# Wide and narrow expert passes, one after the other or mixed unit by unit

## Reference

```python
D_FF_EXPERT = 3584; N_EXPERTS = 8; TOP_K = 2
def swiglu(x, w_gate, w_up, w_down):
    return (jax.nn.silu(x @ w_gate) * (x @ w_up)) @ w_down

def moe_swiglu(x, router_w, w_gate, w_up, w_down):
    logits = (x @ router_w).astype(jnp.float32)
    top_v, top_i = lax.top_k(logits, TOP_K)
    gates = jax.nn.softmax(top_v, axis=-1)
    combine = jnp.sum(jax.nn.one_hot(top_i, N_EXPERTS, dtype=jnp.float32) * gates[..., None], axis=-2)
    y = jnp.zeros_like(x)
    for e in range(N_EXPERTS):
        y = y + combine[..., e:e + 1].astype(x.dtype) * swiglu(x, w_gate[e], w_up[e], w_down[e])
    return y
```

## Time and profile before

| | |
|---|---|
| three runs | 2547.36, 2551.19, 2551.25 us (median 2551.19) |
| profiled execution | 2547.49 us, span 2545.5 us |
| busy: PE, PEld, DVE, ACT | 2435.9, 2106.4, 1891.4, 1407.5 us (96, 83, 74, 55%) |
| DMA | 593.18 MB, mean 233 GB/s |
| chain of waits, by engine | PE 67%, DVE 21%, DMA 5% |
| segment `moe` (seven straight passes) | 1593.7 to 2392.0 us |
| pass 7 in `over` | 2392 to 2528 us |

### The profile page before, as it was taken

How to read it: one execution, slowest core, us unless ns; L and a number is a source line. 1 busy time by engine, 2 the same in 40 slices (tenths; PEclk the granted TensorE clock), 3 DMA queues, 4 the chain that set the end, 5 groups by cost and what they waited for, 6 DMA issues and landing times.

```text
span 2545.5 us, 36256 instructions
## 1 busy us (share of the span) xinstructions
PE 2435.9 (96%) x14462; PEld 2106.4 (83%) x14462; DVE 1891.4 (74%) x2230; ACT 1407.5 (55%) x1546; POOL 0.2 (0%) x4
## 2 busy tenths in 40 slices
PE   7999999999999999989999988999999999999897
PEld 7999889899998998886998886787777777888786
DVE  7665755567657454976544985889999999988787
ACT  4654443456445343223442322678888888777574
POOL 0000000000000000000000000000000000000000
PEclk9999999999999999999999998999999999999998
DMA  6334455344345544304544302899999999999796
GB/s 260 133 117 149 163 217 199 134 156 144 122 153 210 184 166 170 130 34 158 191 165 152 133 17 99 329 362 403 412 413 413 413 411 413 383 342 371 287 354 260
DMA packets 119622, 593.18 MB, mean 233 GB/s; under 512 B 17440, under 2 KB 17824, under 8 KB 77472
## 3 DMA queue, kind: packets, MB, share of 16 engines
q1 hardware_dynamic: 110224, 585.40, 60.4%
q10 hardware_dynamic: 9232, 5.47, 0.8%
HBM read 589.79 MB, written 1.05 MB: 232 GB/s over the span
## 4 chain that ended last, share of the span: by engine, by line
PE 67%; DVE 21%; DMA 5%; issue 4%; ACT 3%; SPq 0%; DVEq 0%; ACTq 0%; POOLq 0%
PE bank L608 21%; PE bank L2508 17%; PE bank L865 12%; DVE wlo L687 7%; DMA ring<-in_stream 4%; PE bank L1717 3%; DVE big L2963 2%; DVE ring_lo L839 2%; PE bank L1133 2%; ACT whi L682 1%; PE bank L1148 1%; PE bank L1738 1%; PE bank L1903 1%; DVE big L2125 1%; PE bank L2448 1%
## 5 line engine op out<-in xcount | busy, mean ns | idle before, releaser
L687 DVE TENSOR_TENSOR wlo<-ring,whi 128x2048 fp32r<-128x2048 f32 x430 | 979.1, 2290 | 112.3 <-ACT whi L682 108.6
L682 ACT ACTIVATE whi<-ring 128x2048 fp32r<-128x2048 f32 x433 | 825.4, 1912 | 109.4 <-PE bank L2508 50.0
L2508 PE MATMUL bank<-whi,xhi 128*128 128x512 f32 x896 | 366.8, 409 | 16.4 <-DVE wlo L687 12.3
L2508 PE MATMUL bank<-wlo,xhi 128*128 128x512 f32 x896 | 352.2, 393 | 0.0
L839 DVE TENSOR_TENSOR ring_lo<-ring,slot_hi 128x1024 fp32r<-128x1024 f32 x160 | 192.4, 1222 | 130.2 <-ACT slot_hi L816 123.1
L608 PE MATMUL bank<-xhi,whi 128*128 128x256 f32 x864 | 245.8, 284 | 2.5 <-DVE xlo L570 1.3
L608 PE MATMUL bank<-xlo,whi 128*128 128x256 f32 x864 | 245.7, 284 | 0.0
L608 PE MATMUL bank<-xhi,wlo 128*128 128x256 f32 x864 | 245.6, 284 | 0.0
L816 ACT ACTIVATE slot_hi<-ring 128x1024 fp32r<-128x1024 f32 x160 | 166.5, 1052 | 107.2 <-PE bank L865 77.6
L2508 PEld LDWEIGHTS bank<-whi,xhi 128*128 128x128 f32 x896 | 170.0, 190 | 63.9 <-DVE wlo L687 30.5
L865 PE MATMUL bank<-xh,slot_hi 128*128 128x256 f32 x704 | 202.5, 288 | 3.0 <-DVE ring_lo L839 3.0
(11 more groups left out here) (524 smaller groups left out, 4505.8 us busy)
## 6 DMA issues: line engine op xcount, KB each, us to landing
ring<-in_stream SPq DMA_DIRECT2D x555, 1024.0 KB, 7.3
par<-in_par ACTq DMA_DIRECT2D x2, 2048.0 KB, 10.0
con<-in_con SPq DMA_DIRECT2D x1, 1216.0 KB, 10.6
X<-in_x SPq DMA_DIRECT2D x2, 512.0 KB, 4.1
out_y<-X SPq DMA_DIRECT2D x2, 512.0 KB, 2.6
par<-in_par ACTq DMA_DIRECT2D x2, 448.0 KB, 6.2
par<-in_par ACTq DMA_DIRECT2D x2, 157.5 KB, 4.4
con<-in_con SPq DMA_DIRECT2D x1, 64.0 KB, 4.3
```

What stands on the lines that cost most here:

```text
L682: act.activation(whi[:, k % NSPLIT, :], src, ACT.Copy).then_inc(act_done, AC.step(tag + f".w{k}"))
L687: v.tensor_tensor(wlo[:, k % NSPLIT, :], src, whi[:, k % NSPLIT, :].bitcast(F32), ALU.subtract)\
L2508: mm = pe.matmul(out, left, right, start=start and i == 0, stop=stop and i == len(pairs) - 1)
```

## The change

`TRACKS` names two tracks, (0, 5, 6, 7) wide and (1, 2, 3, 4) narrow. `straight_units` mixes the units of the two in the segment `moe`: `STRETCHES` gives pairs (wide units, narrow units), and within a pair they are spread evenly. The order of the 98 units (W wide, n narrow) is

The small order work of DVE (`v_order_passes`) moves from units 1 to 3 to units 0, 5 and 7, and the table of experts for SP is written in its first part. The rolled segment keeps its own side work in banks 6 and 7. Core of the diff:

```diff
-WIDE_PASS = (0, 5, 6, 7)
+TRACKS = ((0, 5, 6, 7), (1, 2, 3, 4))
+WIDE_PASS = TRACKS[0]
+STRETCHES = ((5, 0), (9, 9), (4, 5), (5, 14), (5, 4), (7, 10), (7, 3), (0, 11))
...
             def turn(g):
-                if g >= 2:
-                    pe.wait_ge(vec_done, VE.at(tag + (f".hl{g - 2}" if is_wide(g - 2, rolled) else f".h{g - 2}")))
+                if g:
+                    pe.wait_ge(vec_done, VE.at(tag + (f".hl{g - 1}" if is_wide(g - 1, rolled) else f".h{g - 1}")))
...
+            aside_read = []
+
+            def side(kind, p, piece):
+                for done, steps, name in aside_read[-1:]:
+                    pe.wait_ge(done, steps.at(tag + name))
+                name = f".{kind}{p}.{piece}"
+                if kind == "put":
...
+                        mm = pe.transpose(aside[:, t * P:(t + 1) * P], seats_of(p)[:, t, :], ident)
+                    aside_read.append((act_done, AC, name))
+                elif kind == "add":
+                    t, cols = piece // 2, halves(piece % 2)
+                    pe.wait_ge(act_done, AC.at(tag + f".put{p}.0"))
+                    pe.wait_ge(vec_done, VE.at(tag + f"{p}.og"))
+                    pe.matmul(aside, put[:, t, :], og_hi[:, cols], start=True, stop=False)
+                    mm = pe.matmul(aside, put[:, t, :], og_lo[:, cols], start=False, stop=True)
+                    aside_read.append((vec_done, VE, name))
+                else:
+                    pe.wait_ge(vec_done, VE.at(tag + f".seats{p}"))
+                    for k in range(4):
+                        for t in range(NT):
+                            mm = pe.matmul(aside[:, k * CAP:(k + 1) * CAP],
+                                           X[:, t, (4 * piece + k) * P:(4 * piece + k + 1) * P], seats_of(p)[:, t, :],
+                                           start=(t == 0), stop=(t == NT - 1))
+                    aside_read.append((vec_done, VE, name))
...
+                if rolled is None:
+                    for task, q, piece in tasks[g]:
+                        side(task, q, piece)
+                    continue
```

On ACT the reads of a task of unit g-1 stand in the step for up0 of g, behind its split. On DVE they stand in the step for up1 of g, behind its split:

```diff
                 if k + LEAD < n:
                     v_split(v, tag, k + LEAD, rg_)
                 at = tag + str(p)
-                if rolled is None and p == 0 and kind == "up1":
-                    if u == 0:
+                if rolled is None and kind == "up1":
+                    if g:
+                        for task, q, piece in tasks[g - 1]:
+                            side(task, q, piece)
```

More of the change, by code:

```diff
@@ L328, in slot_index, with unit_of @@
             return up, dn
-        straight, over = expert_order(STRAIGHT * UNITS_EXP), expert_order(UNITS_EXP)
+        units = straight_units()
+        tasks, task_at, ended, before_in_track = side_tasks(units)
+        straight, over = expert_order(len(units)), expert_order(UNITS_EXP)
+        track_place = {p: track.index(p) for track in TRACKS for p in track}
+        def unit_of(g, rolled):
+            return units[g] if rolled is None else (0, g)
         def stream_slot(tag, k):
@@ L2511, in up @@
             def up(k, g, first):
-                half = (g // UNITS_EXP) % 2 if rolled is None else rolled
+                half = track_place[units[g][0]] % 2 if rolled is None else rolled
                 cap = slice(half * CAP, (half + 1) * CAP)
@@ new lines, in take_seats @@
+            def take_seats(p):
+                b = before_in_track[p]
+                if b is not None and before_in_track[b] is not None:
+                    v.wait_ge(pe_done, PE.at(tag + f".put{before_in_track[b]}.0"))
+                v_wait(v)
+                for t in range(NT):
+                    if p in WIDE_PASS:
+                        out, numbers = seats_of(p)[:, t, :], c("iota")
+                    else:
+                        out = seats_of(p)[:, t, :].rearrange("p (d c) -> p d c", d=2)
+                        numbers = c("iota")[:, 0:NARROW].unsqueeze(1).to_broadcast([P, 2, NARROW])
+                    v.tensor_scalar(out, numbers, place[:, t, p:p + 1], None, ALU.is_equal)\
+                     .then_inc(vec_done, VE.step(tag + f".seats{p}" if t else None))
@@ L2836, in v_experts @@
-                if kind == "up1" and u in (4, 6) and (p or rolled is not None):
-                    weight = wgt[:, :, p - 1] if rolled is None else wcol
-                    v_scatter(v, at, u // 2 - 2, weight[:, u // 2 - 2:u // 2 - 1])
-                if kind == "up1" and u == 11 and rolled is None:
-                    v_gather(v, at, (p + 1) % 2, p + 1 in WIDE_PASS)
+                    for q in range(2, NEXP):
+                        if task_at[("gather", q, 0)] == g + 1:
+                            take_seats(q)
@@ L2841, in v_experts @@
+                    if g == len(units) - 1:
+                        v.tensor_copy(ccol[:, 0:NT], wgt[:, :, ended[-1]]).then_inc(vec_done, VE.step())
+                if rolled is not None and kind == "up1":
+                    if u == 1:
+                        picks(at)
+                    if u in (4, 6):
+                        v_scatter(v, at, u // 2 - 2, wcol[:, u // 2 - 2:u // 2 - 1])
             if rolled is not None:
-                v_gather(v, tag + "0", rolled, True)
+                v_gather(v, tag + "0", rolled)
```

251 lines of the change are left out of this document (171 added, 80 removed).

## The result

The changed kernel takes 2677.4 us (median of 4 runs, 2675.2 to 2679.2), the kernel before 2550.9; the ratio is 1.050, with a 95% interval of 1.0487 to 1.0513. That is slower, as forecast, and by 126 us instead of 66 to 70: outside the range, and worse than the case that I gave 0.82. The time is in the stage of the straight passes. It ends at 2524.1 instead of 2392, and the last pass behind it takes 135 us (136 before).

The account below looks back on a forecast made before the run. PE, DMA and DVE each need 745 to 748 us of the 798.3 us stage. PE's work 747.6, waits 103 and remainder 17 give stage 868, 70 more: 2547.5 + 70 = 2617.5 us, range 2590 to 2660.

Parts of the forecast that it names:

- the case that I gave 0.82: The forecast itself: stage of the straight passes 70 us longer, kernel time 2617.5 us; chance 0.82.
- PE's own work: Stage of the seven straight expert passes: PE's work summed unit by unit, 747.6 us of 798.3.
- the 50 us to be won: Same stage: PE stands still for 50.7 us, which is all that there is to win.
- The loop and its 33 waits: Shared side bank: PE waits for DVE's read behind a split, 33 times, 103 us; bank free after 5.80 us.
- One turn bank, accumulators, order work: Straight passes: single turn bank has 6 us of cover; moved accumulators and DVE's planner instructions: each costs nothing.
- The clock: PE's granted clock behind the new waits of 2.65 to 3.7 us: taken as nothing, upper end 66 us.
- Case C: Rival, slower still: the clock falls after most waits, 2617.5 + 40 to 66, about 2670 us; chance 0.07.
- The prediction's own last sign: Changed kernel's profile: a lower clock granted in the pairs of tasks means wrong in size, not in mechanism.
- The remainder: Old waits that stay in the 65 units outside the pairs: up to 34 us, taken as 17.
- my 868: Forecast length in us of the stage of the straight passes, 70 us more than 798.3.
- Rival A: Same stage levels out and is faster: 768 to 769 us, kernel time 2517 us; chance 0.08.
- point of decision: For Rival A: an average wait for each pair under 50/33 = 1.5 us wins, above it loses.

Follow-up runs that it names:

- spaced plan: Changed kernel with only the planner edited: it leaves a unit free behind each add or gather where deadlines allow; 2526.7 us, ratio 0.9905.
- the run of 2523 us: Changed kernel with spaced plan, DVE's side-bank read before the split, and PE's task behind the down product; 2523.1 us, ratio 0.9891.
- the early read alone: Changed kernel with one edit on DVE: it reads the side bank before the split, no longer behind it; 2552.6 us, ratio 1.001.
- the task behind the down product: Changed kernel with one edit on PE: a unit's task stands behind its down product, no longer in front; 2565.2 us, ratio 1.0064.
- the two orders with the spaced plan: Changed kernel with spaced plan, units in mixed order (2526.7 us) or in the old order of 14 wide, 56 narrow, 28 wide (2561.8 us).

## Why the prediction was right and wrong

**PE's own work and the 50 us to be won: right.** 747.6 us was the sum. The spaced plan's stage is 777.3 us, 29.7 more. PE's waits in it are 14.5 of these (5.7 for scr before a turn, 5.2 for the side bank, 2.0 at the start), the low clock some 3. About 12 stay open, beside 11.8 us in which weight loads waited for wlo. Of the 50 us to be won, 23 to 28 were.

**The loop and its 33 waits: right,** in place and number, and in size for 29 of them: 106.6 us against 103 in all, 6.0 us against 5.80 for the loop, 3.77 against 3.7 for one pair. The order's rows for DVE and one wide unit of the old trace were enough. The other four, 5.0 to 5.5 us, are 1.5 to 1.9 us above the loop, which leaves out that DVE can itself be behind where the transfers run full. They add 6.6 us and the 29 take 3 off, so that the sum agrees within 4% is partly luck. Putting PE's work inside the loop took it off the waits, as the same formula said. That the four split buffers close the loop was not tested by a run with five; the first row of ACT in the pair shown above speaks for it: ACT stood 5.21 us until PE was done with a slot.

**One turn bank, accumulators, order work: nothing, and right.** All stand in the run of 2523 us, and no wait of a turn for a low part (hlo) stands in the changed kernel's waits.

**The clock: the step that failed.** It reads: "The new waits of 2.65 to 3.7 us are nearer the second, so I take nothing." I had two rows, 1.0 for waits under 1.8 us and 0.5 after 7.84, and picked the near end for waits that lie between. The stage's granted clock came out at 0.93. The price: half of the 109 us in which PE worked at the low level, 54 us, against 5 in the kernel before; by PE's busy time 52.5 us over the spaced plan, which has one such wait (38.7 over the kernel before, whose rows are themselves longer, 775.4 against 761.6); and filling the waits gave 38 us of the run back. Case C ("the clock falls after most waits"), with 40 to 66 us and a chance of 0.07, was what happened; together with the forecast's waits it gave "about 2670", 7 us from the result. The prediction's own last sign, wrong in size and not in mechanism "if a lower clock is granted in the runs of pairs", names this case.

The rows between the two were there to be read. The window of the narrow pass in the earlier trace rows opens 3 us behind a wait of 2.12 us (the longest for og_lo in the earlier trace rows: not all waits are under 1.8), and the clock is 0.50 until 1842; in the mean over 106 us, 1.00, this does not show. In an earlier segment, where the transfers stand still, a wait of 3.80 us has the same behind it. From the trace of the kernel before, each wait and then a window behind it:

```profile
1837.84 0.47 PE L2508 MATMUL bank<-whi,hhi 128*128 128x512 f32 x1 [2.12 <-DVE og_lo L2814]
1839.00:1842.00 3.00, 3.00 (x8) 2.32 (x7) 3.00 (x3) 2.51 (x4) 0.00 (x0) 0.50 1.05 415
```
```profile
1093.83 1.40 PE L1756 MATMUL bank<-con,big 128*128 128x128 f32 x8 [3.80 <-DVE big L2249]
1094.50:1097.50 3.00, 3.00 (x10) 2.54 (x9) 3.00 (x8) 0.00 (x0) 0.00 (x0) 0.50 0.00 0
```

That whole trace has six PE waits of 2.4 to 3.85 us, and the low level stands behind all six. No choice between two ends was needed.

**The remainder: about right.** I took 17 us between 0 and 34. The stage from its first matmul is 928.4 us; less 747.6, 106.6 and the clock's 52.5 that leaves 21.7. So the 62 us that the stage lies above my 868 are the clock (52.5), the waits (3.6), the remainder (some 5) and the 2 us before the first matmul. PE's wait for wlo at the weight loads did fall to 7.7 us, as the prediction said.

**Rival A: wrong as the answer, near in size.** With the waits gone the kernel reaches 2523 to 2527 us, against 2517. Its point of decision, 1.5 us a pair, was too high: the early read alone, with 24.5 us left, 0.7 us for each of the 33 pairs, came out even with the kernel before, and the task behind the down product, with 1.0 us a pair, lost 14 us. The point was worked out from 50 us to be won; with the 23 to 28 that were won it is 0.7 to 0.85.
The Trainium skill, Perfetto Trace Analysis, Optimization Strategy, says that interleaving regimes may improve performance. The trace agrees once the side work does not wait: 35 us between the two orders with the spaced plan. The section's other sentence, that a repeating gap can mean too little PSUM, is not the whole of it here: the bank stayed one, and another plan, or another place of the read, removed most of the gap. Whether a second side bank would have done so too was not tried; all eight are taken.

## What to carry to other kernels

When two engines hand one buffer back and forth, write down what stands between the hand-overs on each engine's program order, and where a wait closes a circle through a third engine, the circle's length less PE's own work inside it is the wait (here 6.0 us less 0.1 for a turn and 1.9 for up1), whatever run-ahead the rings allow. Move the reader to the head of its step before adding buffers: here one split (2.3 us) ahead of a read of 0.75 us cost 125 us in all. And where PE has no slack, count a repeated wait of the length seen here (2.4 us or more) at its length plus what the lower clock costs behind it, and look in the old trace for waits of that length before deciding that the clock holds; one unchanged comparison (the new order with and without the waits) then tells a good idea from the way in which it was built.

## What the runs showed of the hardware

A single wait of 2.4 to 3.8 us on PE in an otherwise dense stretch mostly brings the granted clock down behind it: in the changed kernel behind 22 of the 27 side waits of that length, behind all four longer ones and behind neither of the two of 2.1 us. Waits of about 2 us can do it too, as the 2.12 us one above shows. At 0.50 of 2.4 GHz (1.2 GHz) matmuls of 512 columns start 0.43 us apart instead of 0.23. The window behind the pair shown above, in the changed kernel:

```profile
1851.00:1855.00 4.00, 4.00 (x10) 3.13 (x11) 1.92 (x1) 0.00 (x0) 0.00 (x0) 0.50 1.02 406
```

Matmuls whose result is thrown away, about 1.7 us of them in each wait, kept the stage's clock at 0.99, and the run was 38 us shorter than with PE standing still in their place.
